# A fused decoder layer on one core: x loaded in pieces, gate rounds by tokens, heads four sub-blocks later, two output groups interleaved

## The chip, the cores and the metric

The kernel runs on one core of a Trainium2 chip. TensorE (PE) multiplies, VectorE (DVE) and ScalarE (ACT) do the elementwise work, GpSimd (POOL) sets up constants, and SyncE (SP) issues nearly all DMAs. The metric is the device time of one execution in microseconds (us), as the median over several runs. Lower is better.

## What is computed

One decoder layer on 256 tokens of width 2048: an RMS norm, one input projection for eight mLSTM heads and eight retention heads, the two head mechanisms with a norm and a gate for each head, an output projection with its norm added to x, then a SwiGLU feed-forward with its norm. All in float32.

```python
D_MODEL = 2048; SEQ = 256; HEAD_DIM = 128; CHUNK = 128; D_FF = 5632
h = rmsnorm(x, g_mix_pre)
mq, mk, mv, mo, mi, mf, rq, rk, rv, rg = split(h @ w_in)
qk = silu(causal_dwconv(concat([mq, mk]), conv_w, conv_b))
hm = mlstm_chunkwise(mq, mk, mv, mi + b_igate, mf + b_fgate)
hm = head_rmsnorm(hm, g_mlstm_head) * sigmoid(mo)
hr = retention_chunkwise(rotary(rq), rotary(rk), rv)
hr = head_rmsnorm(hr, g_ret_head) * silu(rg)
x = x + rmsnorm(concat([hm, hr]) @ w_out, g_mix_post)
h = rmsnorm(x, g_ffn_pre)
x = x + rmsnorm((silu(h @ w_gate) * (h @ w_up)) @ w_down, g_ffn_post)
```

## The kernel before

**Products.** Float32 accuracy comes from a split: each weight and each activation is written as a rounded part (`hi`) plus a rest (`lo`), and a product is made of hi*hi, hi*lo and lo*hi. Weights arrive in `raw` (four buffers of 1 MB). ACT copies half a buffer, a sub-block ("sub"), to `w_hi` (line 428), DVE subtracts to get `w_lo` (line 726), and PE multiplies it. `w_hi` and `w_lo` have four slots (`AHEAD`), so ACT starts the copy of sub s+4 when PE has ended sub s, and SP loads a buffer again when DVE has ended its two subs. Eight subs are a round. All engines run the same list of rounds, and the code of each engine goes through `head_step`, the weight step (`ahead` on ACT, `lo` on DVE) and `mixer_step` for each sub, in that order. Every engine works strictly through its own list.

**Two forms.** By tokens (`sub_tokens`), the activation is the stationary operand and the weights move: 12 products of 512 columns in a sub. By columns (`sub_columns`), the weights are stationary and the result comes out transposed: 8 pairs of a product of 512 columns and one of 256, and the two halves of the result must still be added (`copy_right` on ACT, `unit_sums` on DVE).

**Stages.** Start: x is loaded in two DMAs of 1 MB (one for each tile t of 128 tokens), squared and summed, normed to `h0` (line 757), transposed on PE, and split to `hT` (lines 450 and 739). `keep_clock` puts small products on PE meanwhile. Then 4 rounds make the values v. Then 12 rounds (`R_IN` to `R_OUT`) in four groups of three: q, k and gate for four heads each; groups 0 and 1 are mLSTM, 2 and 3 retention. All are in the columns form, a round in two units of four subs. When a unit of q or k ends, DVE adds its halves (line 861) and convolves (lines 880 and 884; groups 0, 1) or rotates (lines 894 to 900; groups 2, 3) it, one half of that work in `mixer_step` of the unit's last sub and one in that of the next sub. A gate unit goes through `unit_sums` to `gT` and a sigmoid on ACT (line 555).

**Heads.** The heads of a group begin in its gate round, one every two subs, and each takes a step every sub: PE `scores`; DVE `weigh`; PE `weighted` after that sub; ACT denominator; DVE `head_recip`; ACT squares; DVE `head_variance`; ACT root; DVE `head_scaled` writes `y`; PE `turned` transposes y into the single bank `B_T`; DVE `mix` (line 946) multiplies by the gate into `gT`; ACT (line 543) and DVE `mix_rest` (line 952) split it into `mixT`. `turned` of a head waits for `mix` of the head before (`mix_ready`), since that frees the bank. `head_at(rnd, s, first)` gives the head whose step stands `first` subs behind its scores. Heads 2 and 3 of a group are turned in the round behind the gate round, which is the next group's q round.

**Output, feed-forward, end.** Four rounds multiply `mixT` by `w_out`, one column group g each, in accumulator pair g % 2; a group's end is squared on ACT and multiplied by a gain on DVE (`emptied`). After the last group, and again at the very end of the kernel, DVE adds the four partial sums of squares and scales them (lines 1002 and 1005), ACT takes a root, and DVE adds the result to `resid`. The feed-forward takes 33 rounds by tokens.

## Time and profile before

| | us |
|---|---|
| median of 3 runs | 1235.66 |
| lowest and highest | 1235.53, 1236.18 |
| the profiled execution | 1235.49 |
| span of its trace | 1233.5 |

In the trace PE is busy for 1219.8 us, DVE for 704.3, ACT for 598.9 and POOL for 12.4; the DMA engines are busy for 63% of the span. The granted PE clock is full throughout. The span of the trace runs from the first to the last instruction; the 1.99 us between it and the execution's own time lie around it.

### The profile page before, as it was taken

The page shows a single profiled execution, that of the slowest core. Times are in us where ns is not written, and L with a number is a line of the kernel's source. Part 1 is how long each engine was busy: PE and PEld are TensorE (multiplying, and loading weights), DVE is VectorE, ACT ScalarE, POOL GpSimd, SP SyncE. Part 2 cuts the span into 40 slices and gives each one's busy share as a digit, 9 for nine tenths or more (in the row PEclk, how much of TensorE's full clock was granted, in tenths as well). Part 3 has the DMA queues.
Part 4 walks back from the last instruction along what each step waited for, and adds up shares of the span by engine and source line. Part 5 has one row for each costly group of instructions (what it writes and reads, how often), then busy time and mean ns, then how long its engine had stood idle before and what let it go on. Part 6 is the DMA issues. An engine that isn't in the chain of part 4 may idle for free.

```text
span 1233.5 us, 15772 instructions
## 1 busy us (share of the span) xinstructions
PE 1219.8 (99%) x5907; PEld 1026.0 (83%) x5907; DVE 704.3 (57%) x898; ACT 598.9 (49%) x781; POOL 12.4 (1%) x35
## 2 busy tenths in 40 slices
PE   8999999999999999999999999999999999999997
PEld 7888888888888888888888888888888888888886
DVE  6656767777676646754554455454455454444444
ACT  5454666574655644644444444444444444343442
POOL 1000100000000000000000000000000000000000
PEclk9999999999999999999999999999999999999999
DMA  8566798967887566455565656565555665555551
GB/s 313 188 157 159 148 214 173 142 181 164 204 178 177 205 204 206 140 200 188 187 189 186 196 178 203 177 197 189 185 188 186 203 208 203 193 184 203 192 183 69
DMA packets 136936, 229.48 MB, mean 186 GB/s; under 512 B 6080, under 2 KB 55488, under 8 KB 136384
## 3 DMA queue, kind: packets, MB, share of 16 engines
q1 hardware_dynamic: 136608, 226.84, 62.9%
q0 software_dynamic: 288, 2.10, 0.5%
q8 instruction: 26, 0.43, 0.1%
q14 instruction: 14, 0.11, 0.0%
HBM read 226.83 MB, written 2.10 MB: 186 GB/s over the span
## 4 chain that ended last, share of the span: by engine, by line
PE 92%; DMA 4%; DVE 2%; ACT 1%; issue 0%; DVEq 0%; SPq 0%; ACTq 0%
PE bank L1142 91%; DMA raw<-in_w_in 3%; PE bank L1386 1%; DVE w_lo L726 1%; ACT w_hi L428 1%; DMA resid<-in_x 0%; DVE h L757 0%; PE bank L1304 0%; PE bank L1147 0%; DVE resid L1014 0%; ACT h L459 0%; PE bank L1359 0%; DVE gT L894 0%; ACT L555 0%; DVE pre L861 0%
## 5 line engine op out<-in xcount | busy, mean ns | idle before, releaser
L726 DVE TENSOR_TENSOR w_lo<-raw,w_hi 128x1024 fp32r<-128x1024 f32 x420 | 513.4, 1225 | 492.3 <-ACT w_hi L428 492.1
L428 ACT ACTIVATE w_hi<-raw 128x1024 fp32r<-128x1024 f32 x420 | 444.0, 1060 | 574.3 <-PE bank L1142 554.9
L1142 PE MATMUL bank<-w_hi,h2T 128*128 128x512 f32 x1376 | 426.6, 390 | 0.0
L1142 PEld LDWEIGHTS bank<-w_hi,h2T 128*128 128x128 f32 x1376 | 258.3, 188 | 53.4
L1142 PE MATMUL bank<-hT,w_hi 128*128 128x512 f32 x768 | 271.3, 397 | 0.0
L1142 PE MATMUL bank<-w_lo,h2T 128*128 128x512 f32 x688 | 267.7, 389 | 0.0
L1142 PE MATMUL bank<-w_hi,ffT 128*128 128x512 f32 x704 | 217.0, 389 | 0.0
L1142 PE MATMUL bank<-hT,w_lo 128*128 128x256 f32 x768 | 214.4, 279 | 0.0
L1142 PEld LDWEIGHTS bank<-hT,w_hi 128*128 128x128 f32 x768 | 144.0, 188 | 32.4
L1142 PEld LDWEIGHTS bank<-w_hi,ffT 128*128 128x128 f32 x704 | 132.2, 188 | 27.4
L1142 PEld LDWEIGHTS bank<-w_lo,h2T 128*128 128x128 f32 x688 | 129.2, 188 | 26.4
L1142 PEld LDWEIGHTS bank<-hT,w_lo 128*128 128x128 f32 x768 | 144.9, 189 | 0.0
L1142 PE MATMUL bank<-w_lo,ffT 128*128 128x512 f32 x352 | 136.9, 389 | 0.0
L1142 PE MATMUL bank<-w_hi,hT 128*128 128x512 f32 x256 | 80.4, 392 | 1.2 <-DVE w_lo L726 1.2
L1142 PE MATMUL bank<-w_hi,mixT 128*128 128x512 f32 x256 | 80.2, 391 | 0.0
L1142 PEld LDWEIGHTS bank<-w_lo,ffT 128*128 128x128 f32 x352 | 66.1, 188 | 13.7
L1142 PEld LDWEIGHTS bank<-w_hi,hT 128*128 128x128 f32 x256 | 48.1, 188 | 11.4 <-issue 1.4
L1142 PEld LDWEIGHTS bank<-w_hi,mixT 128*128 128x128 f32 x256 | 48.1, 188 | 10.4 <-DVE mixT L952 0.4
L1142 PE MATMUL bank<-w_lo,hT 128*128 128x512 f32 x128 | 49.8, 389 | 0.0
L1142 PE MATMUL bank<-w_lo,mixT 128*128 128x512 f32 x128 | 49.8, 389 | 0.0
L1142 PEld LDWEIGHTS bank<-w_lo,hT 128*128 128x128 f32 x128 | 24.1, 188 | 4.8
L1142 PEld LDWEIGHTS bank<-w_lo,mixT 128*128 128x128 f32 x128 | 24.1, 188 | 4.8
(159 smaller groups left out, 549.0 us busy)
## 6 DMA issues: line engine op xcount, KB each, us to landing
raw<-in_w_in SPq DMA_DIRECT2D x63, 1024.0 KB, 12.5
raw<-in_w_gate SPq DMA_DIRECT2D x44, 1024.0 KB, 5.2
raw<-in_w_up SPq DMA_DIRECT2D x44, 1024.0 KB, 5.1
raw<-in_w_down SPq DMA_DIRECT2D x44, 1024.0 KB, 5.0
raw<-in_w_out SPq DMA_DIRECT2D x16, 1024.0 KB, 5.1
resid<-in_x SPq DMA_DIRECT2D x2, 1024.0 KB, 5.9
out<-resid SPq DMA_DIRECT2D x8, 256.0 KB, 2.5
raw<-in_w_in SPq DMA_DIRECT2D x2, 512.0 KB, 8.5
```

The source lines that it names most:

```text
L428: act.activation(w_hi[:, s % AHEAD, :], raw[:, s // 2, (s % 2) * SUB:(s % 2 + 1) * SUB], ACT.Copy).then_inc(hi_done, 1)
L726: dve.tensor_tensor(w_lo[:, s % AHEAD, :], raw[:, s // 2, (s % 2) * SUB:(s % 2 + 1) * SUB], w_hi[:, s % AHEAD, :].bitcast(F32), ALU.subtra ...
L1142: return pe.matmul(out_, lhsT, rhs, start=start, stop=stop, skip_group_check=True)
L1386: ins = pe.transpose(bank[:, B_FF + j // 2, c:c + P], ff[:, t, j * P:(j + 1) * P], ident)
```

## The change

- **x in pieces.** Each tile of x is loaded in three DMAs (1024, 512 and 512 columns) and squared in three steps. DVE makes a bias from the first two sums while the third square runs, and ACT takes the root of (third sum / D + bias) at once. The first weight copy, `hi(0, 0)`, now stands ahead of the first transposed tiles on ACT, `lo(0, 0)` ahead of them on DVE. DVE norms three of eight chunks of h0 ahead of the first sub and the other five between the first weight steps; PE turns one group of four tiles behind its first sub instead of ahead of it.
- **Gate rounds by tokens.** The four gate rounds use `sub_tokens` into one accumulator pair. ACT takes the sigmoid or silu straight from PSUM into `gate_out`, both tiles in one place behind the round's last sub. `head_scaled` multiplies y by the gate in the same instruction as the norm. `mix`, the gate units' sums and copies, and the product at line 977 are gone. The final split to mixT is now read from the bank `B_T` by ACT and by DVE, so that bank is free only when `mix_rest` has run: the turning of the next head waits for `mix_lo`. The gate's weights are loaded in rows of 2 KB, not 1 KB.
- **Heads four subs later** (`HEAD_LAG = 4`): heads 0 and 1 of a group begin in the second half of the gate round, heads 2 and 3 in the first half of the next round. `mix_rest` stands 7 subs behind a head's scores (before: `mix` 6, `mix_rest` 8).
- **Two output groups interleaved**: output groups 0 and 1 are done up to sub 5 first, then the last two subs of each, then group 2.
- **Last roots from sums.** The first three partial sums are added when group 2 ends, and the root takes the fourth square as its input and the rest as its bias, in place of two DVE instructions.

```diff
+HEAD_LAG = 4
+OUT_SUBS = [(0, k) for k in range(6)] + [(1, k) for k in range(6)] + [(0, 6), (0, 7), (1, 6), (1, 7)]\
+    + [(2, k) for k in range(8)]
 def head_at(rnd, s, first):
...
-        n, odd = divmod(8 * (rnd - gate_round(group)) + s - first, 2)
+        n, odd = divmod(8 * (rnd - gate_round(group)) + s - HEAD_LAG - first, 2)
...
+            def last_root(dst, t, part, squares, norm):
+
+                act.wait_ge(bias_ready, norm)
+                act.wait_ge(sq_done, squares)
+                act.activation(dst, stat[:, S_PSQ + 4 * t + part:S_PSQ + 4 * t + part + 1], ACT.Sqrt,
+                               scale=1.0 / D, bias=stat[:, S_PBIAS + t:S_PBIAS + t + 1]).then_inc(sd_ready, 1)
...
+                if is_gate(rnd) and s == 7:
+                    event = event_of(rnd, 0)
+                    act.wait_ge(acc_free, event + 2)
+                    for t in range(TT):
+                        ins = act.activation(gate_out[:, t, :], acc(pair_used(event))[:, t, :],
+                                             ACT.Silu if rnd >= gate_round(2) else ACT.Sigmoid)
+                    ins.then_inc(acc_free, 1)
...
             for s in range(AHEAD):
+                lo(0, s)
                 transposed_lo(hT, C_GPRE, 0, first_bank, start_tiles(s))
-                lo(0, s)
+                if s == 0:
+                    scaled(1, (1,))
+                if s >= 2:
+                    scaled(s - 2, (2, 3))
...
-            def mix(a):
-
-                dve.wait_ge(yT_done, a + 1)
-                dve.wait_ge(gate_sig, a // 2 + 1)
-                dve.scalar_tensor_tensor(gT[:, a % 4, :], bank[:, B_T, 0:SEQ],
-                                         coef[:, C_GHEAD + a:C_GHEAD + a + 1], gT[:, a % 4, :],
-                                         ALU.mult, ALU.mult).then_inc(mix_ready, 1)
 
             def mix_rest(a):
                 dve.wait_ge(mix_hi, a + 1)
-                dve.tensor_tensor(mixT[:, a, SEQ:2 * SEQ], gT[:, a % 4, :],
-                                  mixT[:, a, 0:SEQ].bitcast(F32), ALU.subtract).then_inc(mix_lo, 1)
+                dve.scalar_tensor_tensor(mixT[:, a, SEQ:2 * SEQ], bank[:, B_T, 0:SEQ],
+                                         coef[:, C_GHEAD + a:C_GHEAD + a + 1],
+                                         mixT[:, a, 0:SEQ].bitcast(F32),
+                                         ALU.mult, ALU.subtract).then_inc(mix_lo, 1)
...
-                for step, first in ((weigh, 0), (mix, 6), (head_scaled, 4), (head_variance, 3),
-                                    (head_recip, 2), (mix_rest, 8)):
+                for step, first in ((weigh, 0), (head_scaled, 4), (head_variance, 3), (head_recip, 2),
+                                    (mix_rest, 7)):
...
-            def turned(group, n):
-                pe.wait_ge(y_ready, 4 * group + (n + 3))
-                if n:
-                    pe.wait_ge(mix_ready, 4 * group + n)
+            def head_turned(a):
+                pe.wait_ge(y_ready, a + 3)
+                if a:
+                    pe.wait_ge(mix_lo, a)
```

**Place 1: DVE in the q round behind gate round 0.** Here the heads left over from group 0 meet the work on the first q unit of group 1. Lines 861 and 916 are `unit_sums`, 880/884 and 936/940 the convolution, 726 and 771 the weight step `lo`. Before, from the weight steps of subs 2 and 3 on:

```order
L726 TENSOR_TENSOR w_lo<-raw,w_hi 128x1024 [waits hi_done] x2
L861 TENSOR_TENSOR pre<-bank,right 128x2x256 [waits right_ready]
L880 TENSOR_SCALAR gT<-pre,columns 128x256 [waits acc_free]
L880 TENSOR_SCALAR gT<-pre,columns 128x256
L884 SCALAR_TENSOR_TENSOR gT<-pre,columns,gT 128x256 [waits dve_step] x2
L946 SCALAR_TENSOR_TENSOR gT<-bank,columns,gT 128x256 [waits gate_sig,yT_done]
L952 TENSOR_TENSOR mixT<-gT,mixT 128x256 [waits mix_hi]
L726 TENSOR_TENSOR w_lo<-raw,w_hi 128x1024 [waits hi_done]
L884 SCALAR_TENSOR_TENSOR gT<-pre,columns,gT 128x256 [waits dve_step] x2
L884 SCALAR_TENSOR_TENSOR pre<-pre,columns,gT 128x256 [waits dve_step] x2
```

In the changed kernel, from the second convolution step of sub 3 on (line 1003 is `mix_rest`, here of head 1):

```order
L940 SCALAR_TENSOR_TENSOR spin<-pre,columns,spin 128x256 [waits dve_step] x2
L988 RECIPROCAL stat<-stat 128x2 [waits sd_ready]
L989 TENSOR_TENSOR stat<-stat 128x2 [waits dve_step]
L995 SCALAR_TENSOR_TENSOR y<-bank,stat,gate_out 128x128 [waits acc_free,yT_done,dve_step]
L995 SCALAR_TENSOR_TENSOR y<-bank,stat,gate_out 128x128
L978 TENSOR_TENSOR stat<-stat,floor 128x2 [waits den_ready]
L979 RECIPROCAL stat<-stat 128x2 [waits dve_step]
L771 TENSOR_TENSOR w_lo<-raw,w_hi 128x1024 [waits hi_done]
L940 SCALAR_TENSOR_TENSOR spin<-pre,columns,spin 128x256 [waits dve_step] x2
L940 SCALAR_TENSOR_TENSOR pre<-pre,columns,spin 128x256 [waits dve_step] x2
L983 TENSOR_SCALAR stat<-stat 128x2 [waits sq_done]
L1003 SCALAR_TENSOR_TENSOR mixT<-bank,columns,mixT 128x256 [waits mix_hi]
```

The steps of heads 2 and 3 (`head_scaled`, `head_recip`, `head_variance`) now stand between the halves of the convolution and behind it, and `mix_rest` of head 1 stands behind them all.

**Place 2: PE behind sub 5 of that same q round** (line 1350 is `head_turned`, here of head 2). In the changed kernel, the end of sub 5, the turning, and the beginning of sub 6:

```order
L1188 MATMUL bank<-hT,w_hi 128x512
L1188 MATMUL bank<-hT,w_lo 128x256
L1350 MATMUL bank<-columns,y 128x128 [waits mix_lo,y_ready]
L1350 MATMUL bank<-columns,y 128x128
L1188 MATMUL bank<-hT,w_hi 128x512 [waits lo_done]
L1188 MATMUL bank<-hT,w_lo 128x256
```

Before, the same head was turned behind sub 1 of the q round, and waited for `mix` of head 1, a step ahead of its `mix_rest`:

```order
L1304 MATMUL bank<-columns,y 128x128 [waits mix_ready,y_ready]
L1304 MATMUL bank<-columns,y 128x128
L1155 REGISTER_ALU
L1142 MATMUL bank<-hT,w_hi 128x512 [waits lo_done]
L1142 MATMUL bank<-hT,w_lo 128x256
```

What moved is the place of the turning, four subs later, and the step it waits for.

**Place 3: ACT at the end of gate round 0** (line 455 is `hi`, 593 the gate, 471 the root of head 0, 576 a denominator). In the changed kernel:

```order
L455 ACTIVATE w_hi<-raw 128x1024
L593 ACT_TABLE_LOAD
L593 ACTIVATE gate_out<-bank 128x512 x2
L471 ACT_TABLE_LOAD
L471 ACTIVATE stat<-stat 128x2
L576 ACTIVATE stat<-bank 128x2
L455 ACTIVATE w_hi<-raw 128x1024
```

The gate and two loads of function tables now stand ahead of the root of head 0, which before had one load ahead of it.

## Rows read from the trace of the kernel before

**Rows 1.** The page, busy us of each engine and share of the span.
```profile
PE 1219.8 (99%) x5907; PEld 1026.0 (83%) x5907; DVE 704.3 (57%) x898; ACT 598.9 (49%) x781; POOL 12.4 (1%) x35
```

**Rows 2.** The waits: engine, tile and line, releaser: us in total, times, longest.
```profile
PE bank L1142 <- DVE probs L912: 1.2, 2, 0.9
PEld bank L1304 <- DVE y L938: 0.7, 2, 0.5
PEld bank L1142 <- DVE mixT L952: 0.4, 1, 0.4
```

**Rows 3.** The chain that ended last, in order of time: start, us, what.
```profile
27.52 0.44 PE bank L1147 x4
...
547.65 43.57 PE bank L1142 x192
```

**Rows 4.** Windows, 12 uninterrupted subs by columns: busy us, clock, DMA share, GB/s.
```profile
197.32:230.69 33.37, 33.37 (x195) 29.43 (x194) 27.02 (x43) 17.68 (x20) 0.00 (x0) 1.00 0.99 176
```

**Rows 5.** Timeline of the start: start us, us, engine, line, instruction, idle before.
```profile
5.73 1.91 ACT L459 ACTIVATE h<-resid 128x2048 f32<-128x2048 f32 x1 [3.42 <-DMA resid<-in_x]
...
9.48 1.04 PE L1147 MATMUL bank<-columns,h 128*128 128x128 f32 x8
...
10.36 1.06 PE L1142 MATMUL bank<-columns 128*128 128x128 f32 x8
...
12.11 1.26 PE L1147 MATMUL bank<-columns,h 128*128 128x128 f32 x8 [0.69 <-DVE h L757]
12.65 0.84 ACT L450 ACTIVATE hT<-bank,columns 128x256 fp32r<-128x256 f32 x2 [1.49 <-PE bank L1147]
...
13.71 0.91 DVE L739 SCALAR_TENSOR_TENSOR hT<-bank,columns,hT 128x256 fp32r<-128x256 f32 x2
...
15.89 0.47 PE L1142 MATMUL bank<-w_hi,hT 128*128 128x512 f32 x1 [1.19 <-DVE w_lo L726]
```

**Rows 6.** The tile of x, first 14 us: its two DMAs, issue to landing.
```profile
DMA to landing us min/median/max: 4.9/5.9/7.0
```

**Rows 7.** Timeline, q round behind gate round 0, from the end of sub 3.
```profile
197.18 0.38 PE L1304 MATMUL bank<-columns,y 128*128 128x128 f32 x2
...
198.48 1.23 DVE L726 TENSOR_TENSOR w_lo<-raw,w_hi 128x1024 fp32r<-128x1024 f32 x1 [0.51 <-ACT w_hi L428]
...
201.78 0.48 DVE L946 SCALAR_TENSOR_TENSOR gT<-bank,columns,gT 128x256 f32<-128x256 f32 x1
...
202.51 1.22 DVE L726 TENSOR_TENSOR w_lo<-raw,w_hi 128x1024 fp32r<-128x1024 f32 x1
...
205.23 1.23 DVE L726 TENSOR_TENSOR w_lo<-raw,w_hi 128x1024 fp32r<-128x1024 f32 x1
```

**Rows 8.** Timeline, q round behind gate round 1, from the end of sub 3.
```profile
270.06 0.38 PE L1304 MATMUL bank<-columns,y 128*128 128x128 f32 x2
...
277.70 1.22 DVE L726 TENSOR_TENSOR w_lo<-raw,w_hi 128x1024 fp32r<-128x1024 f32 x1
```

**Rows 9.** Timeline, one head in gate round 0: ACT's table load and root, DVE's head_scaled.
```profile
172.57 1.28 ACT L444 ACT_TABLE_LOAD   x1
...
173.86 0.20 ACT L444 ACTIVATE stat<-stat 128x2 f32<-128x2 f32 x1
...
174.81 0.61 DVE L938 TENSOR_SCALAR y<-bank,stat 128x128 f32<-128x128 f32 x2
```

**Rows 10.** Timeline of PE in gate round 0, its first `weighted`.
```profile
163.83 0.93 PE L1142 MATMUL bank<-v_sb,probs 128*128 x6 [0.91 <-DVE probs L912]
```

**Rows 11.** Timeline of the kernel's end, DVE and ACT.
```profile
1226.67 0.16 DVE L1002 TENSOR_REDUCE stat<-stat 128x1 f32<-128x4 f32 x1 [1.45 <-ACT bank L598]
...
1226.93 0.68 DVE L1007 TENSOR_TENSOR ff_out<-bank,g_post 128x512 f32<-128x512 f32 x1
```

**Rows 12.** Lines: instructions, count, busy us, mean ns of one; ACT from PSUM.
```profile
L659 ACT ACTIVATE ff<-bank,stat 128x512 f32<-128x512 f32 x22 | 13.7, 675 | 0.0
```

**Rows 13.** Windows, the stretch behind the last product, columns as in Rows 4.
```profile
1226.00:1233.50 7.50, 0.00 (x0) 0.00 (x0) 3.81 (x8) 0.84 (x3) 0.00 (x0) 0.80 0.53 188
```

More of the change, by code:

```diff
@@ L61 @@
 E_IN = 2
-E_OUT = E_IN + 24
+E_OUT = E_IN + 20
 E_FF = E_OUT + 4
@@ L1164, in sub_columns, with unit_columns @@
                 ins.then_inc(sub_done, 1)
-            def unit_columns(rnd, unit, event, act_T, before=None, after=None):
+            def unit_columns(rnd, unit, act_T, before, after):
+                event = event_of(rnd, unit)
                 pe.wait_ge(acc_free, event + 1)
@@ L1233, in _ @@
             keep_clock(4, 1)
-            for c in range(2):
-                start_transposed(1, c)
+            start_transposed(1, 0)
             keep_clock(6, 1)
@@ L1305, in turned @@
                 ins.then_inc(yT_done, 1)
-            def gate_units(group, rnd, event):
-                def before(s):
-                    if s % 2 == 0:
-                        scores(group, s // 2)
-                def after(s):
-                    if s % 2 == 1:
-                        weighted(group, s // 2)
-                        if s >= 5:
-                            turned(group, (s - 5) // 2)
-                for u in range(2):
-                    unit_columns(rnd, u, event + u, hT, before, after)
@@ L1344, in _, with heads_in_front @@
-            for g in range(4):
-                pe.wait_ge(acc_free, E_OUT + g + 1)
-                for s in range(8 if g < 3 else 8 - SPLIT_OUT):
-                    if g == 0:
-                        pe.wait_ge(mix_lo, 2 * s + 2)
-                    sub_tokens(8 * (R_OUT + g) + s + 1, s % AHEAD, mixT, g % 2, 2 * s, KT - 1)
-                    if g == 0:
-                        left_over(3)(s)
+            def heads_in_front(rnd, s):
+                a = head_at(rnd, s, 0)
+                if a is not None:
+                    scores(a)
@@ new lines, in heads_behind @@
+            def heads_behind(rnd, s):
+                for step, first in ((weighted, 1), (head_turned, 5)):
+                    a = head_at(rnd, s, first)
+                    if a is not None:
+                        step(a)
+                if (rnd, s) == (R_IN, 3):
+                    pe.wait_ge(gates_act, 1)
+                    pe.wait_ge(gates_dve, 2)
+                if (rnd, s) == (R_IN, 6):
+                    gate_columns()
+                if rnd == R_IN + 1 and s == 0:
+                    spread_rows()
```

258 lines of the change are left out of this document (138 added, 120 removed).

## The prediction

> **What bounds the kernel now.** I read the page's busy shares first. PE is busy for 1219.8 of 1233.5 us [rows 1], so only three things can shorten the kernel: PE starting earlier, PE doing its work in less time, or PE waiting less. DVE (57%) and ACT (49%) matter only where PE waits for them. The list of waits, next, says where that is: 1.2 us for DVE's `probs` in two waits, 0.7 us for `y`, 0.4 us for `mixT` [rows 2]. Third, the chain that ended last is almost all PE, and gives its pace: 192 products of the tokens form in 43.57 us, 0.227 us each, so 2.72 us a sub [rows 3]. The window over 12 uninterrupted subs by columns gives 33.37 us, 2.78 us a sub [rows 4]. Last come the timelines of the places that the change touches: the start, the q round behind a gate round, the end [rows 5, 7, 8, 11]. There the reader is to see not PE, which runs on, but how late DVE is against PE's sub: its slack is what the change spends.
>
> **Start.** x0 lands at 5.7, and 1.91 us of squaring follow [rows 5]. In three pieces, two of them are squared while the rest arrives, and the root of tile 0 comes about 0.9 us earlier, at 7.3. Tile 1, which lands at about 1.2 + 7.0 = 8.2 [rows 6], takes three squares, some 2.6 us with their fixed parts, so its root comes at about 10.1 and its first chunk of h0 at about 11.0. Six issues for x instead of two put the weights' DMAs later in SP's queue, by four issues of some 0.4 us, but the bytes of x lie ahead of them in either kernel. So what is late next is PE itself: its fillers last until 9.48, eight transposes and eight more fillers follow (10.36 + 1.06), and the four transposes of tile 1 begin at about 11.3 instead of 12.11 [rows 5]. ACT's first hT comes 0.54 later (12.65 behind 12.11), so at 11.85, its pair ends at 12.7; `lo(0, 0)` is already done, as its copy waits only for the first weights (0.5 MB behind x; at x's own pace, 1 MB from 5.7 to 8.2, they land at 9.5, and I allow 10.7). One DVE step of 0.46 us (half of 0.91) and 0.15 us to PE's start put the first product at 13.35 instead of 15.89: 2.5 us. Four transposes (0.44 us [rows 3]) that were hidden ahead of the first sub now lie on PE behind it, at 0.36 to 0.44. Net **-2.2 us** (-3.0 to -1.0, the latter if the weights land at 11.8). The five chunks of h0 that move behind the first sub (about 0.6 us each) keep DVE busy, but by the same rows it has `lo` for sub 4 about 0.8 us before PE asks.
>
> **Gate rounds by tokens.** 32 subs go from 2.78 to 2.72 us [rows 3, 4]: **-1.7 us**. Ends: -1.9, and -0.8 if the refill after each head's products costs the tokens form more. The heads' own products are the same in number. The 8 unit sums, the sigmoids on gT and the 16 `mix` that vanish were off PE's path and pay only through the waits below.
>
> **Waits that go.** `weighted` of head 0 waited 0.91 us for `probs` [rows 10], since `weigh` stood behind the unit sums of the k round; with heads four subs later it does not. With the other waits of rows 2 that is 2.3 us; by the distances from one head's products to the next, which catch short waits too, 2.6. I take **-2.5** (-2.6 to -1.2).
>
> **Gate taken on ACT in one place.** From the end of the gate round's last sub: the weight copy is done 1.3 later (198.48 less 197.18 [rows 7]); table load 1.29 (173.86 less 172.57) to 2.6; two gate instructions of some 0.6 to 0.68 [rows 12] to 3.85; the second load to 5.1; root of head 0 (0.20) to 5.3; two small DVE steps, some 0.4, and y, 0.61 [rows 9], to 6.4. PE needs y of head 0 when it has done one `weighted`, one `scores` (some 0.65 each) and two subs (5.6): 6.9. So nothing is lost, with 0.5 us to spare: **0** (0 to +1 over four groups). The price hangs on the load: were ACT to stand as long again behind each, y would come 2.6 us later and PE would wait 2.1 in each of four groups, +8.4. Rows 9 show nothing of the kind. The Trainium skill (ScalarE: Activation LUTs, What ACT_TABLE_LOAD costs) gives a drain of 1380 ns with every switch; by it the sum would be some 9 us higher. Here the trace does not agree, for the root follows its load at 1.29 us.
>
> **The new wait: `turned` for `mix_rest`.** This is the largest term. Before, head 2's turning waited for `mix` of head 1, which DVE did a sub earlier. Now it stands behind sub 5 of the q round and waits for `mix_rest` of head 1, which DVE reaches in that same sub, behind the convolution of the first q unit. Rows 7 give DVE's time without the new steps: from PE's end of sub 3 (197.18), DVE's weight step begins 1.30 later, and the second half of the convolution ends at 205.23, 8.05 later. That stretch held `mix` and `mix_rest` for 0.73 us (201.78 to 202.51), which go; `head_scaled` and `head_recip`, about 1.2 us, come in their place: 8.5. Behind it come `head_variance` (about 0.15) and `mix_rest`, now of the form that takes 0.46 to 0.5 us [rows 5]: 9.2. PE does `weighted` and `turned` (0.8) and two subs (5.6) and asks at 6.4. It waits **2.7 us** after gate round 0. DVE has the same slack in the other groups with rotation: 277.70 - 270.06 = 7.64 [rows 8], so 8.75, a wait of 2.3 us twice: **4.6**. Behind sub 7, head 3's turning waits for head 2's `mix_rest`, behind one weight step: 1.3 + 1.2 + 0.5 = 3.0 against a sub of 2.78, **0.2** three times, 0.6. After gate round 3 there is no convolution: waits of 0.4 and 0.25 at the same two places, **0.6**. Sum **+8.5 us** (+7.0 to +10). What is queued behind the waiting transposes is all of PE's work. Nothing gives it back, since PE is the bound.
>
> **Interleaved output groups.** Group 2's first product needs the pair that group 0 emptied. DVE ends that about 3.7 us after group 0's last sub (weight step 1.3 + 1.2, two products of 0.68, one of which is in [rows 11]); PE comes after two subs, 5.4. Cost 0. **Last roots.** At the end 1226.67 to 1226.93 goes [rows 11]: -0.26; the same before the feed-forward, where PE waits at the second tile: -0.3. Together **-0.5** (-0.7 to -0.2).
>
> **The sum.** -2.2 - 1.7 - 2.5 + 0 + 8.5 - 0.5 = +1.6 us. On the profiled execution's 1235.49 that is 1237.1. The median of the runs is 0.17 above that execution, so I forecast **1237.2 us**, 0.13% slower. About 0.2%, 2.5 us, is what a measurement of this kernel can tell from no change.
>
> **Rivals.**
> - *The turning does not wait, or hardly* (1228 to 1231): if DVE's order were kinder than I read it, or its steps ran closer, the term of 8.5 falls to 0 to 2, and 1228.7 is left. Against it: DVE's list is strict and the 8.05 us are measured in the same place. 14 in 100.
> - *The wait is there but smaller, or the start gives more* (1231.5 to 1235): 11 in 100.
> - *Slower by more* (1240 to 1245), one mechanism: late weights in the q round. In rows 4 the DMA share is 0.99 at 176 GB/s, where two subs (1.05 MB in 5.56 us) ask for 189. If the weights of the sub between the convolution's halves are late, DVE's `lo` waits there and `mix_rest` behind it. Their copy normally ends 4.9 after sub 3's end and DVE asks at 5.9, so it decides once it is over 1 us late, and from there goes one to one into PE's wait. At 3 us beyond that, in two of three groups, it gives 1237 + 6 = 1243. The gate rounds' 2 KB rows relieve the queues; the copies of rows 7 were on time. 11 in 100.
> - *The clock falls in the pauses.* Behind the last product, with PE idle for 7.5 us, the granted clock averages 0.80 of 2.4 GHz [rows 13]; with PE at work it is 1.00 [rows 4]. At half speed (1.2 GHz), one sub after each of three pauses would cost 2.7 us more: 1245. The pauses are shorter than that stretch, whose mean is still nearer to full. 3 in 100. The Trainium skill (TensorE: Matmul & The Clock Gate, Why this matters for your kernels) warns of idle gaps between bursts of products; no row here has one in the middle of the work.
> - *ACT stands longer behind a table load*, as worked out above: 1237 + 8.4 = 1245.6. 1 in 100, since rows 9 show it not to.
>
> **How the numbers follow.** The forecast's own case (1235 to 1239.8: the bounds of its terms, which don't all fall on one side) has 60 in 100. The range 1230.5 to 1242.5 leaves out most of the first rival (11), a third of the third (4) and the last two (4), 19 in 100. Faster by over 0.2% is below 1233.2: 14 and half of 11, 0.20. Slower is above 1238.1: 11 + 3 + 1 and a third of the forecast's case, 0.35. The rest is 0.45.
>
> **What would show it.** Right: in the list of waits, PE on `y` transposes waits for DVE `mixT` about 2.7, 2.3 and 2.3 us, once a group, and short ones beside; the first 128x512 product starts at about 13.4; `probs` is gone as a releaser; 12 products every 2.72 us in gate rounds. Wrong: no such wait, then the time is near 1229; a wait for `y` behind sub 1 of the q rounds, then ACT's gate place costs; PE clock below 1.00 behind a pause.

## The result and the profile after

| | before | after |
|---|---|---|
| median of the runs, us | 1235.92 | 1255.09 |
| lowest and highest, us | 1235.53, 1236.78 | 1253.54, 1256.90 |
| the profiled execution, us | 1235.49 | 1256.63 |
| span of its trace, us | 1233.5 | 1254.3 |

The changed kernel takes 1.0149 of the time of the kernel before, with a 95% interval of 1.0134 to 1.0164: 19 us slower. The forecast was 1237.2 with a range of 1230.5 to 1242.5, so the time lies far outside.

The page of the changed kernel gives PE's share, as in [rows 1]. PE's busy time has grown by 7 us, and the idle time by 14. The same work is done, so part of it runs more slowly.

```profile
PE 1226.9 (98%) x5779; PEld 1023.8 (82%) x5779; DVE 690.8 (55%) x868; ACT 585.6 (47%) x773; POOL 12.4 (1%) x35
```

The list of waits of PE answers [rows 2]. `probs` and `y` are gone, as forecast. `mixT` stands for 7.3 us. What I had not forecast is `w_lo` and `floor` (the copy of the mLSTM gate columns out of PSUM, on which the spread products wait).

```profile
PE bank L1350 <- DVE mixT L1003: 7.3, 5, 2.6
PE bank L1188 <- DVE w_lo L771: 5.6, 4, 4.3
...
PE bank L1188 <- DVE floor L908: 2.6, 1, 2.6
PE bank L1188 <- DVE hT L784: 0.9, 1, 0.9
```

Both come from ACT, which waits for weights: 19.4 us in 7 waits before, 34.9 in 9 after, by ACT's own list.

```profile
ACT w_hi L455 <- DMA raw<-in_w_in: 34.9, 9, 7.7
```

The windows below have the columns of [rows 4] and begin and end at PE's subs. They show, in this order:

1. the pause ahead of the spread product,
2. the sub behind that product, at a mean clock of 0.62 (4.45 us instead of 2.78),
3. the next sub, at full clock,
4. the pause for `w_lo`,
5. the sub behind it, at 0.62,
6. and 7. the subs behind the first two waits of the turning (0.63 each),
8. the sub behind the third such wait (1.00, 2.90 us),
9. six uninterrupted subs by columns.

```profile
134.68:137.43 2.75, 0.16 (x3) 0.04 (x1) 1.54 (x4) 2.49 (x3) 0.00 (x0) 1.00 0.88 130
139.49:143.94 4.45, 4.45 (x17) 3.84 (x17) 1.09 (x3) 0.00 (x0) 0.00 (x0) 0.62 0.74 99
143.94:146.72 2.78, 2.78 (x19) 2.45 (x17) 0.80 (x1) 1.89 (x2) 0.00 (x0) 1.00 0.69 119
154.90:159.51 4.61, 0.31 (x3) 0.01 (x1) 1.22 (x1) 2.34 (x3) 0.00 (x0) 1.00 0.95 157
159.51:163.98 4.47, 4.47 (x16) 3.79 (x17) 1.41 (x2) 4.47 (x13) 1.88 (x8) 0.62 0.80 168
214.84:219.22 4.38, 4.38 (x18) 3.76 (x17) 1.69 (x5) 2.18 (x4) 0.00 (x0) 0.63 0.60 165
292.08:296.39 4.31, 4.31 (x19) 3.69 (x17) 1.66 (x5) 0.51 (x2) 0.00 (x0) 0.63 0.90 136
369.98:372.88 2.90, 2.90 (x19) 2.53 (x18) 1.66 (x5) 0.51 (x2) 0.00 (x0) 1.00 0.34 88
225.35:242.31 16.96, 16.96 (x98) 14.71 (x97) 14.01 (x24) 9.29 (x10) 0.00 (x0) 1.00 0.64 186
```

So four subs run partly at half speed (1.2 instead of 2.4 GHz), which costs 1.4 to 1.7 us each.

The q round behind gate round 0, which [rows 7] show before, is here DVE's timeline. From the end of PE's sub 3 at about 205.5, the second half of the convolution ends at 214.0, and `mix_rest` of head 1 (line 1003) at 214.5. PE has been waiting since 212.0 and turns at 214.60.

```profile
210.41 0.61 DVE L995 SCALAR_TENSOR_TENSOR y<-bank,stat,gate_out 128x128 f32<-128x128 f32 x2
...
211.21 1.20 DVE L771 TENSOR_TENSOR w_lo<-raw,w_hi 128x1024 fp32r<-128x1024 f32 x1
212.33 0.87 DVE L940 SCALAR_TENSOR_TENSOR spin<-pre,columns,spin 128x256 f32<-128x256 f32 x2
213.12 0.88 DVE L940 SCALAR_TENSOR_TENSOR pre<-pre,columns,spin 128x256 f32<-128x256 f32 x2
213.91 0.16 DVE L983 TENSOR_SCALAR stat<-stat 128x2 f32<-128x2 f32 x1
213.98 0.48 DVE L1003 SCALAR_TENSOR_TENSOR mixT<-bank,columns,mixT 128x256 fp32r<-128x256 f32 x1
```

**Where the 21 us are.** PE's products can be counted off sub by sub in both traces. At the last sub of the v rounds the changed kernel is 0.28 us late, at the first sub of group 0's k round 0.30, and at the end of that round, where the gate round starts, 10.28. Groups 0 to 2 add 3.6, 4.3 and 2.7 (each from its gate round's start to the next one's). At F, as I call the feed-forward's first product by `w_hi`, the difference is 21.34 us: 529.77 against 508.43. Behind F nothing more is lost, and 0.5 us come back. So half of the loss lies in one round that the change does not touch.

### The profile page after: what moved, and what is told of

It reads as the page before. It is cut to its first block, busy times and chain, and to the rows that moved or that the text cites. A ratio compares the mean times of both kernels' runs of the same rounds, so it can differ in the third digit from the quotient of the medians.

```text
span 1254.3 us, 15287 instructions
## 1 busy us (share of the span) xinstructions
PE 1226.9 (98%) x5779; PEld 1023.8 (82%) x5779; DVE 690.8 (55%) x868; ACT 585.6 (47%) x773; POOL 12.4 (1%) x35
## 4 chain that ended last, share of the span: by engine, by line
PE 88%; DMA 5%; DVE 4%; ACT 1%; issue 0%; SPq 0%; DVEq 0%; ACTq 0%
PE bank L1188 86%; DMA raw<-in_w_in 5%; DVE w_lo L771 2%; ACT w_hi L455 1%; PE bank L1428 1%; PE bank L1350 0%; PE bank L1193 0%; DVE spin L950 0%; SPq L347 0%; DVE pre L916 0%; DVE h L798 0%; DVE spin L940 0%; DVE hT L784 0%; DVE resid L1061 0%; DVE mixT L1003 0%
## 5 line engine op out<-in xcount | busy, mean ns | idle before, releaser
L1188 PE MATMUL bank<-hT,w_hi 128*128 128x512 f32 x512 | 188.2, 410 | 4.3 <-DVE w_lo L771 4.3
L1188 PE MATMUL bank<-w_hi,hT 128*128 128x512 f32 x512 | 163.1, 393 | 2.1 <-DVE w_lo L771 1.3
L1188 PE MATMUL bank<-hT,w_lo 128*128 128x256 f32 x512 | 146.0, 285 | 0.0
L1188 PEld LDWEIGHTS bank<-hT,w_hi 128*128 128x128 f32 x512 | 99.1, 194 | 28.3 <-DVE w_lo L771 4.6
L1188 PEld LDWEIGHTS bank<-w_hi,hT 128*128 128x128 f32 x512 | 96.1, 188 | 23.9 <-issue 1.8
L1188 PEld LDWEIGHTS bank<-hT,w_lo 128*128 128x128 f32 x512 | 99.7, 195 | 0.0
L1188 PE MATMUL bank<-w_lo,hT 128*128 128x512 f32 x256 | 99.7, 389 | 0.0
L1188 PEld LDWEIGHTS bank<-w_lo,hT 128*128 128x128 f32 x256 | 48.1, 188 | 9.2
## 6 DMA issues: line engine op xcount, KB each, us to landing
raw<-in_w_in SPq DMA_DIRECT2D x63, 1024.0 KB, 11.3
```

The source lines that it names most:

```text
L1188: return pe.matmul(out_, lhsT, rhs, start=start, stop=stop, skip_group_check=True)
```

## The experiments

The weight loads are numbered in the order in which SP issues them (the first megabyte comes as two halves, 0 and 1, the others as 1 MB each): 17 to 20 are group 0's q round, 21 to 24 its k round, 25 to 28 its gate round. From load 9 to load 24 both kernels issue the same loads, at most 0.3 us apart. The columns are the runs' median, its ratio to the kernel before run beside it, the time from issue to landing of loads 17 and 24, and the time of F. "Other" marks a kernel whose loads have another size. Landings and F are those of the profiled execution; in e7, e10 and e15 it lies 2.1, 4.3 and 2.8 us from the median. e7, e8 and e17 leave out work and do not compute the layer; e17 ran once.

| kernel | us | ratio | load 17 | load 24 | F |
|---|---|---|---|---|---|
| before | 1235.92 | 1 | 12.9 | 12.5 | 508.43 |
| after | 1255.09 | 1.0149 | 7.6 | 31.9 | 529.77 |
| e1 after, head 2 turned elsewhere | 1248.08 | 1.0089 | 7.8 | 31.0 | 521.64 |
| e2 after, old start | 1258.83 | 1.0182 | 7.7 | 31.4 | 531.09 |
| e3 before, new start | 1235.15 | 0.9993 | 13.0 | 13.6 | 508.01 |
| e4 after, fillers | 1255.59 | 1.0151 | 7.6 | 31.1 | 529.00 |
| e5 after, w_in declared last | 1255.97 | 1.0154 | 7.6 | 31.1 | 528.00 |
| e6 before, PE's loop written out | 1252.19 | 1.0126 | 7.4 | 26.6 | 525.79 |
| e7 after, half weights | 1244.38 | 1.0068 | other | other | 516.05 |
| e8 e7 and e1 | 1231.14 | 0.9966 | other | other | 504.80 |
| e9 after, other rows | 1255.28 | 1.0165 | 10.1 | 29.1 | 528.69 |
| e10 e9 and e1 | 1249.18 | 1.0099 | 11.2 | 29.0 | 518.70 |
| e11 before, GpSimd's program longer | 1235.50 | 0.9995 | 12.8 | 11.7 | 509.88 |
| e12 before, other rows | 1244.41 | 1.0069 | 12.4 | 20.0 | 518.59 |
| e13 before, PE's program longer | 1426.93 | 1.1536 | 7.5 | 25.6 | 525.25 |
| e14 before, one pass written out | 1236.04 | 0.9994 | 12.7 | 13.4 | 509.96 |
| e15 e1, loads in halves | 1237.20 | 1.0006 | other | other | 513.77 |
| e16 e3, loads in halves | 1234.28 | 0.9982 | other | other | 508.36 |
| e17 after, PE's program shorter | 1133.14 | - | 12.9 | 13.0 | 518.50 |
| e18 e15, first loads whole | 1235.67 | 1.0007 | other | other | 509.48 |

Load 24 in the views of the queue by issue (KB, and us to landing), in the kernel before, the changed kernel, e13 and e17:

```profile
raw<-in_w_in SPq DMA_DIRECT2D x1, 1024.0 KB, 12.5
raw<-in_w_in SPq DMA_DIRECT2D x1, 1024.0 KB, 31.9
raw<-in_w_in SPq DMA_DIRECT2D x1, 1024.0 KB, 25.6
raw<-in_w_in SPq DMA_DIRECT2D x1, 1024.0 KB, 13.0
```

**Theory and rivals.** The first theory: 7.3 us are the wait for `mix_rest`, 10 us are weights that land late, and the slow clock comes from both pauses. Rivals: the new start upsets the transfers; the clock falls for another reason; DVE or ACT is late by itself.

**e1: the new wait taken away.** Head 2 of each group is turned into the bank of the scores, free by then.

```diff
+        def turned_out(a):
+            return bank[:, B_S if a % 4 == 2 else B_T, 0:SEQ]
...
+                if a and n == 0:
+                    pe.wait_ge(mix_lo, a)
...
-                if a:
+                if a % 4 == 3:
+                    pe.wait_ge(mix_lo, a - 1)
+                elif a and a % 4 != 2:
```

> The changed kernel, but head 2 of each group is turned into the bank of the scores, which is free then, so no turning waits for the mix_rest just before it. In the trace of the changed kernel those waits are 2.57, 2.18, 2.17, 0.24 and 0.18 us, and the granted clock is at half behind the first two. Theory (each wait stands on PE's path, and the half clock behind it is caused by it): 7.3 us of waits and 2 x 1.5 us of slow clock go, 1255.1 - 10.3 = 1244.8. Rival 1 (the clock falls for another reason): only the waits go, 1247.8. Rival 2 (late weights or DVE take over what the waits give back): 1252 or more. The late weights of group 0's q and k rounds stand ahead of this place and should be in the trace unchanged.

Measured: 1248.08, 7.0 less. PE's list has no `mixT` any more, and a new wait of 4.8 for `w_lo` in group 2.

```profile
PE bank L1191 <- DVE w_lo L774: 8.9, 2, 4.8
...
PE bank L1191 <- DVE floor L911: 2.0, 1, 2.0
```

At the start of group 2's gate round the gain over the changed kernel has shrunk to 3.6 us (318.74 against 322.34), of which 1.6 stem from the start; at F it is 8.1. So the waits were on the path, the slow clock behind two of them went, and late weights took a part back: rival 2, in part.

**e4: is it idleness that lowers the clock?**

```diff
+                if a % 4 == 2 and a < 14:
+                    keep_clock(16, B_S)
                 if a:
                     pe.wait_ge(mix_lo, a)
```

> The changed kernel with 16 small products on PE (about 2 us at full clock) ahead of the turning of head 2 in groups 0 to 2, in the time in which PE waits there (2.57, 2.18 and 2.17 us). If the half clock behind these pauses comes from PE standing idle, the two stretches of half clock there go and the time falls by about 2 x 1.5 us, to 1252. If it comes from something else, the clock falls as before and the time is 1255 or, by what the products cost, up to 1 us more.

Measured: 1255.59, no gain. But the clock behind the filled pause is at full speed, and the sub there takes 2.90 us, not 4.38:

```profile
213.13:216.03 2.90, 2.90 (x20) 2.53 (x18) 0.96 (x5) 1.46 (x3) 0.00 (x0) 1.00 0.33 121
```

The timeline shows why nothing is left of it. The sixteen small products (each has two records) take 3.6 us, which is longer than the pause was. From the end of sub 5 to the end of sub 6 it is 6.61 us in all three groups; in the changed kernel it was 7.35, 6.86 and 5.40. The sum is the same: what the clock gives back in two groups, the longer stay costs. I had taken 2 us by reading the counts of [rows 5] as one record a product:

```profile
209.42 3.73 PE L1188 MATMUL bank<-columns 128*128 128x128 f32 x32
212.99 0.38 PE L1352 MATMUL bank<-columns,y 128*128 128x128 f32 x2
```

So the price of a pause here is its length and often 1.5 us of half clock. Not every pause is followed by the second part: six kernels have these three pauses as they are (the changed one, e2, e5, e7, e9, e17), and in their traces the clock fell at the end of 13 of the 18 or in the sub behind; with the fillers it did so at none of three. Idle PE is thus a cause, but not the only one. In e3, e8, e11, e14 and e17 the clock falls just the same behind the spread product (sixteen products of 8 rows and 256 columns), at 136 to 138 us, where PE was busy throughout (30.00 of the 30 us from 110 to 140).

**e2 and e3: does the start set the transfers off?** e2 gives the changed kernel the old start, e3 the kernel before the new one.

> The changed kernel with the start of the kernel before (x in two DMAs, root by way of a variance, old order of the first stage). Theory A (the start gains nothing, and has nothing to do with the late weights of group 0's q and k rounds): first product at 15.9, the v rounds end 0.3 us earlier than in the changed kernel, the waits of 2.6 and 4.3 us for weights stay, 1255 +- 1. Theory B (the six pieces of x and the shifted start set the transfers into the slow pattern that makes the weights late): both waits and the two stretches of half clock behind them go, some 10 us, 1244 to 1246. Rival (the slow pattern comes and goes with every build): anything between, with other loads slow.

> The kernel before with the new start alone. Forecast by the trace of the changed kernel: first product at 13.7, the gain of 2.2 us lost by sub 4, +0.3 us at the end of the v rounds: 1236.2. Theory B (the new start makes weights late in group 0's q and k rounds): 1242 to 1246 with waits of PE for w_lo there. Theory A: no such waits.

Measured: e2 1258.83, with the late weights of the changed kernel (load 24: 31.4); e3 1235.15, without (13.6). The start has nothing to do with them: theory A. It does not even cost anything: the changed kernel is 3.7 us slower without it. At the last v sub the kernels with the new start and whole loads are early, by 0.9 (e3), 1.4 (e1), 1.7 (e4), 1.3 (e5) and 0.4 (e17), and only the profiled execution of the changed kernel is late, by 0.28. There the third load, issued at 5.44, landed only after 12.5 us; in e1 it took 9.6, in e4 9.4.

**e7 and e8: are late weights the rest?** The loads of q and k bring only half their rows, e8 adds e1's edit.

```diff
+                                load(6 * kind + 3 * half + (R_IN + n), q, src)
                             else:
-                                src = in_rows(8 * (q % 2), 8, col + (q // 2) * 256, 256)
-                            load(6 * kind + 3 * half + (R_IN + n), q, src)
+                                src = in_rows(8 * (q % 2), 4, col + (q // 2) * 256, 256)
+                                load(6 * kind + 3 * half + (R_IN + n), q, src, width=SUB)
```

> The changed kernel, but each load of the q and k rounds brings four of its eight rows of each partition, and the second sub of each buffer keeps old values (the result is then not the layer's). Theory (PE's waits ahead of the spread product and in the k round of group 0 are late weights, and the half clock behind them comes from those pauses): 2.6 + 1.6 + 4.4 + 1.6 + 0.4 in group 0 and 0.4 in group 2 go, 1255.1 - 11 = 1244. The waits for mixT (7.3 us) stay. Rival (DVE or ACT is late there by itself): 1250 or more.

> Both together: half of the q and k weights, and head 2 turned into a place of its own. What is left is the change without late weights and without the new wait. By the trace of the changed kernel: 1255.1 - 11 - 10.3 = 1233.8. By the prediction's own terms (start -2.2, tokens -1.7, old waits -2.5, roots -0.5): 1228.8. A time near the second says that those four gains are real and that the loss lies in the two things removed alone; a time near 1234 says that some of them are missing too.

Measured: 1244.38 and 1231.14. The first is the theory's number. The second, 0.9966 (0.9948 to 0.9984), says that without the two things the change would gain some 4 us (2 to 6 by the interval), against 6.9 by the prediction's terms: the gains are real, and smaller than forecast. Halved loads also leave more room in the queue than loads in time would, so the 4 us may flatter it.

**e5: does w_in's place decide?**

> The changed kernel, with w_in declared last among its inputs instead of fourth; no engine's instruction changes. Up to 125 us the kernels before and after issue the same loads at the same times (0.3 us apart), yet in all of the changed kernel's kin load 17 takes 7.6 us and load 24 takes 31 us from issue to landing, in all of the kernel before's kin 12.9 and 12.5 to 13.6. Theory (where w_in lies in memory sets which loads are slow): the landing times of loads 17 to 27 change, and with them the waits of 2.6 and 4.3 us; time 1244 to 1260 without a sign that I can give. Rival (the pattern comes from the program's own order of work): landings as in the changed kernel to 0.5 us and 1255 +- 1.

Measured: 1255.97, landings as in the changed kernel. The order of the declarations plays no part.

**e6: PE's loop.** Comparing the diff again, one edit was left. The kernel before runs PE's first three head groups in a loop; the changed kernel writes them out, since the accumulator pair now alternates from group to group. PE's program grows from 6708 to 8166 instructions. e6 makes that edit alone, in the kernel before (8421):

```diff
-            with pe.Fori(0, 3) as j:
+            for j in range(3):
```

> The kernel before, with PE's loop over the first three head groups written out, so that PE's program is longer, as it is in the changed kernel; the same work in the same order. Theory (the length of the program places things otherwise in memory, and so sets the pattern of slow loads): load 17 lands in about 7.6 instead of 12.9 us and load 24 in some 30 instead of 12.5, weights late in group 0, 1244 or more. Rival: nothing changes, 1236 +- 1.

Measured: 1252.19, 1.0126 (1.0110 to 1.0143). The same products in the same order take 16 us more, and the loads land nearly as in the changed kernel. ACT's list, where the kernel before has 19.4 in 7:

```profile
ACT w_hi L428 <- DMA raw<-in_w_in: 52.7, 14, 8.4
```

This is the cause that I had missed. Load 17 already takes 7.4 instead of 12.9 us. It is issued at 81 us, when PE is in the v rounds, whose code is the same in both.

**e11, e13, e14: length or form?** e11 lengthens GpSimd's program from 88 to 1728 instructions (its edit has 1640 memsets, where the text below says 820). e13 pads PE's program behind its last product with waits that are long fulfilled; two of them make one instruction, so 3426 waits make 8422 in all; e14 writes out one pass of the loop (7587).

```diff
+            for _ in range(3426):
+                pe.wait_ge(consts, 1)
```

> The kernel before, with GpSimd's program longer by 1640 instructions (820 memsets of one column, each waiting for the last), which it runs through between the last head and the load of the last gain, when it has nothing else to do. PE's program with its loop written out is longer by 1713. Theory (the length of the whole program moves things in memory, and that sets the pattern of slow loads): load 17 lands in 7.5 us and load 24 in 25 to 31, and the time is near 1252. Rival (it is PE's program alone): landings as before, 12.9 and 12.5, and 1236.

> The kernel before, with its PE loop kept and 1714 instructions that do nothing (waits that are long fulfilled) behind PE's last product, so that PE's program is as long as with the loop written out (8422 against 8421 instructions). The time is longer by what PE takes for them at the end; what is looked at is the landing of loads 17 to 27 and PE's waits up to 1226 us. Theory L (the length of PE's program sets the pattern of slow loads): load 17 in 7.5 us, load 24 in 25 to 31. Theory F (the written-out form does, or what PE runs there): landings as before, 12.9 and 12.5.

> The kernel before, with one of the three passes of PE's loop written out and two looped (7587 instructions on PE). Up to the end of group 0 and of group 1's k round PE then runs the same code as with all three written out. Theory F: the late weights of group 0 come as in e6 (1252.2), while those of group 2 (6.3 of its 16 us) may not: 1245 to 1252. Theory L: a pattern of its own, any time between 1236 and 1252, load 17 not at 7.5.

Measured: e11 and e14 are the kernel before (1235.50, 1236.04; 12.8 and 12.7 us). e13 takes 191 us more, some 174 of them in the padding at the end, but in front of it the trace is near e6's: load 17 in 7.5, load 24 in 25.6, F at 525.25. The padding is not reached before PE's last product ends, at 1242.7 us. The window from 80 to 160 us, columns as before, shows it: PE is busy throughout in e11, for 76.78 us in e13 and for 78.28 in e6, and the transfer rate falls from 151 to 136 GB/s at a higher DMA share. In e11:

```profile
80.00:160.00 80.00, 80.00 (x416) 67.84 (x415) 52.31 (x77) 43.31 (x61) 5.64 (x16) 0.98 0.74 151
```

In e13:

```profile
80.00:160.00 80.00, 76.78 (x403) 64.53 (x402) 46.82 (x70) 37.55 (x54) 3.60 (x13) 1.00 0.80 136
```

In e6:

```profile
80.00:160.00 80.00, 78.28 (x396) 66.00 (x395) 45.82 (x67) 36.01 (x51) 2.82 (x11) 0.96 0.81 136
```

So it is the length of PE's program, not the form in which the loop is written, and it is neither GpSimd's length nor that of all programs together (e11 adds 1640 instructions in all, e13 adds 1714). ACT's and DVE's programs I did not lengthen. Somewhere between 7587 and 8162 instructions the pattern of slow loads changes.

Two more things are in the traces. The loading of the instructions does not itself crowd out the weights: between 86 and 128 us the instruction queue brings one piece of 16 KB in the kernel before, the changed kernel, e6, e11 and e13 alike. And the pattern is there long before load 17. The load of 128 KB for the mLSTM gate columns, issued at 28 to 33 us, takes 15.0 to 19.6 us in all kernels with up to 7587 PE instructions and 7.7 to 9.2 us in all those with 8162 or more. There it is the short program that has the slow load, so a long one is not slow as such; it moves the slow places to where this kernel has nothing in hand. That load in the kernel before and in e6:

```profile
wg<-in_w_in SPq DMA_DIRECT2D x1, 128.0 KB, 19.1
wg<-in_w_in SPq DMA_DIRECT2D x1, 128.0 KB, 7.7
```

**e17: the reverse test in the changed kernel.** Half of the down projection's products are left out, which makes PE's program 7158 instructions long and leaves all before it as it is.

```diff
-                    sub_tokens(8 * R_DOWN + n + 1, n % AHEAD, ffT, g % 2, 2 * s, KF - 1)
+                    sub_tokens(8 * R_DOWN + n + 1, n % AHEAD, ffT, g % 2, 2 * s, KF - 1, (1,))
```

> The changed kernel with half of the products of the down projection left out on PE (tile 0 of all but the last four subs of the last column group; the result is then not the layer's). That is behind the place of interest, and makes PE's program 7158 instructions long instead of 8166, shorter than the 7587 that still gave the kernel before's pattern. Read is the trace up to the first sub of the feed-forward, which stands at 529.8 us in the changed kernel and at 508.4 in the kernel before. Theory (the length of PE's program sets which loads are slow): load 17 lands in 12.9 us and load 24 in 12 to 14, PE waits for no weights in group 0, and that sub comes at 518 to 521. Rival (the pattern belongs to the changed kernel for another reason): load 24 in 31, the sub at 528 to 530.

Measured, in one execution: load 17 in 12.9, load 24 in 13.0, F at 518.50, 11.3 us earlier than in the changed kernel, 0.7 of which stem from the start. The window and PE's waits of this kernel:

```profile
80.00:160.00 80.00, 80.00 (x414) 67.76 (x413) 52.57 (x78) 43.43 (x61) 5.64 (x16) 0.98 0.73 160
```

```profile
PE bank L1350 <- DVE mixT L1003: 7.4, 5, 2.6
...
PE bank L1188 <- DVE w_lo L771: 1.0, 2, 0.5
```

The changed kernel in the same window, for comparison:

```profile
80.00:160.00 80.00, 73.11 (x376) 61.71 (x375) 43.19 (x63) 30.88 (x38) 0.00 (x0) 0.98 0.82 128
```

**e9, e10, e12: the distance between rows.** In the packets' records most pieces of 1 KB take 46 ns, and in a slow stretch a quarter of them over some 150; the queue then moves some 100 pieces in a microsecond, in a fast stretch 200. Neighbouring partitions read 525,312 bytes apart. The other assignment of rows makes that 32,832.

```diff
-            w_in_rows = w_in.rearrange("(p k) c -> p k c", k=KT)
+            w_in_rows = w_in.rearrange("(k p) c -> p k c", p=P)
```

> The changed kernel with another assignment of w_in's rows to partitions: row 128k + p goes to partition p in place of row 16p + k. The bytes and the pieces of 1 KB stay; what changes is the distance in memory between what neighbouring partitions read, 32,832 bytes instead of 16 x 32,832 = 525,312. (The gain of the first norm is then turned on PE.) Theory (the slow loads come from that distance): a load of the q and k rounds lands in 5 to 6 us as those of the feed-forward do, nobody waits for weights, and the time is that of the run with half of the weights, 1244. Rival (pieces of 1 KB are slow wherever they lie): loads of 10 us stay and the time is 1255 +- 2.

> The same, and head 2 turned into a bank of its own. Theory: both losses go, as in the run with half of the weights and two places, which took 1231.1; so 1231, faster than both kernels. Rival (half the bytes mattered, not the rows): 1244 or more.

> The kernel before with the other assignment of w_in's rows. The kernel before waits 1.2 us for w_lo in one place. Theory: slow loads vanish (load 17 in 5 to 6 us, not 12.9), the time falls by 0 to 1.5 us, to 1235. Rival: the pattern of 12.9 and 10 us stays.

Measured: 1255.28, 1249.18, and 1244.41 for the kernel before. The theory falls. Loads of 10 us and more stay, only others are slow now; the kernel before even loses 8 us by it. The Trainium skill (DMA: Bandwidth & Descriptors, Latency and other measured facts) gives copies a lower rate when their rows lie a large power of two apart: 207 GB/s at 512 KiB and 103 at 4 MiB, against 214 once 4 KiB are added to the latter. What neighbouring partitions read of w_in lay 1 KiB beyond 512 KiB apart, and here the shorter distance brought nothing.

**e15, e16, e18: living with late weights.** Each load is issued as two halves, each as soon as its half of the buffer is free.

```diff
-                    sp.wait_ge(lo_done, 8 * (rnd - 1) + 2 * q + 2)
...
+                for n in range(2):
+                    if wait:
+                        sp.wait_ge(lo_done, 8 * (rnd - 1) + 2 * q + n + 1)
+                    sp.dma_start(raw[:, q, SUB * n:SUB * (n + 1)].rearrange("p (k c) -> p k c", k=k),
+                                 src[:, k * n:k * (n + 1)]).then_inc(raw_full[2 * q + n], 16)
```

> The changed kernel with head 2 turned into a place of its own (1248.1 so far), and every load of 1 MB issued as two of 0.5 MB, each as soon as its own half of the buffer is free and each waited for by itself. The first half is then issued one sub (2.8 us) earlier and its copy waits for half the bytes. Theory (PE's remaining losses are late weights: waits of 2.0, 4.1 and 4.8 us and the slow clock behind them): most of 16 us goes, 1233 to 1240. Rival (the queue's pace is what limits, halves change nothing): 1246 to 1250.

> The kernel before with the new start and with loads in halves. It waits for late weights at one place for 1.2 us and for probs for 1.2. Expected 1233.5 to 1235.5 against 1235.2 with the new start alone; if the finer loads cost SP or the queue something, 1236 or more.

> The changed kernel with head 2 turned into a place of its own and loads in halves, but the first round's loads whole as before: in halves they made PE wait 2.5 us for hT in the start (the end of the v rounds stood at +2.6 us against -1.4 to -1.9 with whole ones). Theory: 1237.2 - 4 = 1233.2, faster than both kernels by 0.2%. Rival (the start's 4 us are eaten by late weights behind it): 1237.

Measured: e15 1237.20, 11 us less than e1, so most of the late weights can be hidden. e18 1235.67: the start's gain is there (the last v sub 1.8 us early), but of the 4 us that I expected nothing is left in the ratio. It is 1.0007 (0.9998 to 1.0016) against 1.0006 in e15; the two medians differ by 1.5 us, but so do, by 1.2, those of the kernel before that ran beside them. PE still waits 3.0 us for `w_lo` in three places, the longest 2.0. e16, the kernel before with the new start and loads in halves, has the lowest ratio of those that compute the layer: 1234.28, 0.9982 (0.9972 to 0.9993).

## Why the prediction was wrong

The terms, as the prediction put them, at F unless said otherwise:

| term | forecast | measured |
|---|---|---|
| start | -2.2 | -0.9 to -1.9 in most traces, -0.4 in e17, +0.3 in the changed kernel's own profile |
| gate rounds by tokens, old waits | -1.7, -2.5 | -3.5 together (e8) |
| gate on ACT in one place | 0 | 0, no wait for y |
| `turned` for `mix_rest` | +8.5 | +7.3 |
| interleaved groups | 0 | 0 |
| last roots | -0.5 | -0.25 at the end, nothing ahead of the feed-forward |
| clock behind the new waits | 0 (a rival, 3 in 100) | +3.0, two stretches of 1.5 |
| PE's loop written out | not seen | +10.6 by late weights and the pauses' slow clock (after less e17, without the start's 0.7) |

How -3.5 comes out: e8's F is 3.63 ahead of the kernel before; 1.64 of that are the start, and a stretch of half clock behind the spread product cost it 1.5. The table adds up to 0.3 - 3.5 + 7.3 + 3.0 + 10.6 = 17.7, and with the same stretch behind the spread product (1.5) to 19.2 of 21.3. The stretch is no doing of the change: e3, e11 and e14, which derive from the kernel before, have it too; the profiled execution of the kernel before has not. Of the remaining 2 us, 1.0 are the small waits for `w_lo` in e17; the last microsecond I have not placed. The whole uninterrupted sub by columns takes 2.83 us in the changed kernel's k round of group 1 (16.96 for six) against 2.78 in [rows 4], for which I have no cause. One sum of the prediction was off: 32 subs at 2.78 less 2.72 us make 1.9, not 1.7; by that the forecast would have been 0.2 us lower.

**The step that failed** is a sentence in "Gate rounds by tokens": "The heads' own products are the same in number." It was true of the products, but I took PE's program for the products. The diff shows the loop over groups replaced by straight code, and I priced it at nothing without saying so; the runs put +10.6 us in its place (and 16 us in e6, where it is the only edit). No row of the trace before could have given its price: the trace has only one length. What I could have read is how little the weights had in hand. ACT already waited 19.4 us for `w_in` in the kernel before, and the third rival said that the queue ran at a DMA share of 0.99. I looked for late weights where my own chain needed them, in the q rounds behind a gate round, gave that 11 in 100, and left out the k round of group 0, where they came. That rival's mechanism (late weights that end up in PE's waits) and its sign were right; its place and its cause were not.

**The new wait was right.** DVE's list was added up from [rows 7] to 9.2 us behind sub 3's end, the trace has about 8.9; the waits are 2.57, 2.18 and 2.17 against 2.7, 2.3 and 2.3, and 0.24 and 0.18 against 0.4 and 0.25 at the end. The three of 0.2 at sub 7 did not come.

**The clock was mis-weighed.** I had the mechanism, priced it at 2.7 us a sub (1.5 measured, and in two of three places), and gave it 3 in 100, since "The pauses are shorter than that stretch, whose mean is still nearer to full." A pause of 7.5 us with a mean of 0.80 says nothing on how short a pause may be. In the changed kernel pauses of 2.2, 2.6, 2.6 and 4.3 us were each followed by a stretch at half speed, another of 2.2 was not. The Trainium skill (TensorE: Matmul & The Clock Gate, Why this matters for your kernels) warns of idle gaps between bursts of products; the traces agree with it, and I should have given its warning more than I did.

**The start** came out smaller. The first product stands at 13.70 against 13.35 forecast. The weights behind it decide what is kept: in the profile of the changed kernel the third load landed at 17.98 and took the gain away (chain of the start, in order of time):

```profile
5.44 12.54 DMA raw<-in_w_in
...
18.00 1.07 ACT w_hi L455
```

**The last roots** did at the end what [rows 11] promised. From the read of the sum to the last addition it is now 1247.79 to 1248.94, 1.15 us, against 1.40 before:

```profile
1247.79 0.19 ACT L637 ACTIVATION_READ_ACCUMULATOR bank<-bank 128x1 f32 x1
1248.01 0.69 DVE L1054 TENSOR_TENSOR ff_out<-bank,g_post 128x512 f32<-128x512 f32 x1 [1.70 <-ACT bank L637]
...
1248.94 0.75 DVE L1061 SCALAR_TENSOR_TENSOR resid<-ff_out,stat,resid 128x512 f32<-128x512 f32 x1
```

## What to carry to other kernels

Count as an edit everything that changes a program's length, also where the work stays the same; before pricing such a change by its arithmetic, run the kernel before with that edit alone. A wait of 2 to 3 us on TensorE costs its length and, in most cases here, a stretch at half clock behind it. Where transfers run with little in hand, a first gain elsewhere is paid back there: issue loads in the pieces in which they are waited for (11 us here), and look at the landing times load by load, not at the mean share.

## What the runs showed of the hardware

- The length of PE's program changes which loads are slow, by up to 19 us for one load of 1 MB, and does so long before PE reaches the added part (e13: load 17 at 81 us, the padding behind 1242 us). 6708, 7158 and 7587 instructions gave one pattern, 8162 to 8422 another, in every profiled execution of either kernel with w_in's rows as they were; 1640 more instructions on GpSimd changed nothing. The Trainium skill (Runtime: NRT & Kernel Launch, Instruction fetch mechanics) has instructions stream in by themselves at a cost that is mostly hidden; here the longer program cost 16 us (e6), and it came through the weights. How the length reaches the transfers is open: I tested where w_in is declared (e5, no effect) and how its rows lie (e9, e12, another pattern again), and no more.
- Loads in pieces of 1 KB run at some 100 or some 200 GB/s in stretches, and when those stretches come depends on that pattern; the feed-forward's loads, in pieces of 2 KB, landed in 5.0 to 5.2 us for 1 MB (medians of before and after).
- Small products on PE (128x128) took 3.6 us for sixteen, 0.22 us each, as long as one with 512 columns by [rows 3].
